# A conditioning matrix times two vectors, beside a two-block transformer on one core: 128x128 tiles with an fp32r split, or row chunks of 2048 columns in plain fp32

## What is computed

```python
silu_c = jax.nn.silu(c)                    # 1024 values
silu_cc = jax.nn.silu(c_ctx)               # 1024 values
for i in range(DEPTH):                     # 2
    mod_x = (silu_c @ w_mod[i] + b_mod[i])[:, None, :]     # w_mod[i] is 1024 x 3072
    mod_c = silu_cc @ w_mod[i] + b_mod[i]
    sh_x, sc_x, g_x = jnp.split(mod_x, 3, axis=-1)
    hx = rms_norm_2(x, norm_g[i]) * (1.0 + sc_x) + sh_x
    ...
    x = x + g_x * yx
```

## Time and profile before

| what | value |
|---|---|
| three runs | 1326.38, 1327.18, 1327.38 us; median 1327.18 us |
| profiled execution, first to last instruction | 1325.0 us (its own time outside the span is not listed; the median of the runs is 2.2 us above the span) |
| PE busy | 1271.4 us, 96% of the span |
| DVE, ACT, POOL busy | 945.7, 723.9, 391.0 us |
| chain that ended last | PE 78%, DVE 9%, ACT 7%, issue 3% |
| mean DMA rate | 145 GB/s |

### The profile page before, as it was taken

One profiled execution on the slowest core, in us unless ns is written; L12 is line 12 of the kernel. 1 busy time (PEld: TensorE's weight loads), 2 busy tenths in 40 slices (PEclk: granted clock), 3 DMA queues, 4 the chain that ended last, 5 costly groups with the idle time before them and its releaser, 6 DMA issues.

```text
span 1325.0 us, 24391 instructions
## 1 busy us (share of the span) xinstructions
PE 1271.4 (96%) x8908; PEld 1102.8 (83%) x8908; DVE 945.7 (71%) x1426; ACT 723.9 (55%) x1257; POOL 391.0 (30%) x377
## 2 busy tenths in 40 slices
PE   5999999999999999999999999999989999999996
PEld 4887899999999877898999998888855699987666
DVE  6878588888878985558988887853377548454674
ACT  5555455655567777545565657644366515413562
POOL 4942144545431140143445452011012320000022
PEclk9999999999999999999999999999999999999999
DMA  8565246666645542155576663322200274522100
GB/s 309 178 218 191 72 141 233 219 222 219 217 154 172 160 130 96 63 191 171 197 234 211 230 213 128 130 93 95 96 1 1 59 181 133 170 95 80 48 1 32
DMA packets 52665, 191.72 MB, mean 145 GB/s; under 512 B 6048, under 2 KB 6304, under 8 KB 52320
## 3 DMA queue, kind: packets, MB, share of 16 engines
q1 hardware_dynamic: 43488, 158.59, 36.2%
q0 software_dynamic: 8368, 31.33, 7.5%
q10 hardware_dynamic: 720, 0.57, 0.2%
HBM read 189.41 MB, written 1.05 MB: 144 GB/s over the span
## 4 chain that ended last, share of the span: by engine, by line
PE 78%; DVE 9%; ACT 7%; issue 3%; POOL 1%; DMA 1%; SPq 0%; DVEq 0%; ACTq 0%; POOLq 0%
PE G L417 13%; PE G L419 13%; PE G L418 13%; PE A L417 6%; PE A L419 6%; PE A L418 6%; DVE WL L1131 3%; PE R L651 3%; PE R L578 2%; PE R L558 2%; ACT WH L1848 2%; PE A L999 1%; PE R L417 1%; PE R L419 1%; PE R L418 1%
## 5 line engine op out<-in xcount | busy, mean ns | idle before, releaser
L1131 DVE TENSOR_TENSOR WL<-RAW,WH 128x1024 fp32r<-128x1024 f32 x295 | 390.4, 1330 | 245.3 <-ACT WH L1848 244.9
L1848 ACT ACTIVATE WH<-RAW 128x1024 fp32r<-128x1024 f32 x295 | 310.4, 1057 | 387.1 <-PE G L419 275.9
L417 PE MATMUL G<-XH,WH 128*128 128x256 f32 (+1 forms) x1336 | 398.7, 298 | 7.8 <-DVE WL L1131 4.6
L419 PE MATMUL G<-XH,WL 128*128 128x256 f32 (+1 forms) x1336 | 395.4, 296 | 0.0
L418 PE MATMUL G<-XL,WH 128*128 128x256 f32 (+1 forms) x1336 | 395.4, 296 | 0.0
L417 PEld LDWEIGHTS G<-XH,WH 128*128 128x128 f32 x1336 | 255.5, 191 | 21.6 <-issue 10.6
L418 PEld LDWEIGHTS G<-XL,WH 128*128 128x128 f32 x1336 | 255.6, 191 | 7.4
L419 PEld LDWEIGHTS G<-XH,WL 128*128 128x128 f32 x1336 | 255.7, 191 | 6.2
L417 PE MATMUL A<-HH,WH 128*128 128x256 f32 x352 | 99.9, 284 | 1.0 <-POOL HL L2477 1.0
L418 PE MATMUL A<-HL,WH 128*128 128x256 f32 x352 | 99.8, 283 | 0.0
L419 PE MATMUL A<-HH,WL 128*128 128x256 f32 x352 | 99.7, 283 | 0.0
(11 more groups left out here) (355 smaller groups left out, 2532.0 us busy)
## 6 DMA issues: line engine op xcount, KB each, us to landing
RAW<-in_wst SPq DMA_DIRECT2D x295, 512.0 KB, 4.1
M<-in_wmod POOLq DMA_DIRECT2D x48, 512.0 KB, 4.1
B<-in_rpb POOLq DMA_DIRECT2D x4, 1024.0 KB, 12.6
H<-in_x_t SPq DMA_DIRECT2D x2, 512.0 KB, 8.4
M<-in_x_tok SPq DMA_DIRECT2D x1, 1024.0 KB, 13.5
M<-in_ctx_t POOLq DMA_DIRECT2D x1, 1024.0 KB, 5.2
out_y<-M SPq DMA_DIRECT2D x2, 384.0 KB, 2.7
C<-in_cst SPq DMA_DIRECT2D x1, 737.0 KB, 15.1
```

Source lines behind the costliest of these rows:

```text
L417: mm(out, lh, rh, start=start, stop=False, skip_group_check=True)
L419: return mm(out, ll, rh, start=False, stop=stop, skip_group_check=True)
L1131: v.tensor_tensor(WL[:, slot, :], RAW[:, raw, :], WH[:, slot, :].bitcast(F32), ALU.subtract).then_inc(w_lo, 1)
L1848: act(WH[:, slot, :], RAW[:, raw, :], ACT.Copy).then_inc(w_hi, 1)
```

## The change

The matrix is cut in another way: 24 chunks of 128 rows by 2048 columns (1 MB each), eight to a third of the columns. A chunk is multiplied by four plain fp32 products of 512 columns, all with the same 128x32 vector, product g into the 32 array columns of group g (`modulate`). Eight chunks add up in `O` and give 2048 output columns.

- First attention: 8 chunks in place of 128 small products. Two stand ahead of the attention, one each in steps 2, 4, 6, 8, 10 and 12; none around the `heads_turn`. `RM` now has three slots of 1 MB.
- FFNs: 8 chunks each in place of 16 `refill`: one after tile 6, 8, 10, 12, 14, 16, 18 and 20. `SCR`, `RH`, `RL`, `YR`, and with them `high`, `row`, `rest`, are gone. Before each load POOL copies the chunk's vector (128x32) from `SC` to `SV`, so that PE can read it at a fixed address in its loop.
- After each FFN: one ACT copy of all of `O` and four transposes of 128 columns, instead of 16 small ones and a sum on DVE.

```diff
@@ program @@
-        SCR = sb("SCR", [P, KD, 32], F32R)
+        SV = sb("SV", [P, 2, 32])
-        RM = mv[:, 6144:12288].rearrange("p (s c) -> p s c", s=RMS)
+        RM = mv[:, 6144:12288].rearrange("p (s g c) -> p s g c", s=RMS, g=4)
@@ block.tensor @@
+            def modulate(vectors, buf, start, stop):
+                for g in range(4):
+                    m = mm(O[32 * g:32 * g + 32, :], vectors, RM[:, buf, g, :], start=start, stop=stop, skip_group_check=True)
+                m.then_inc(m_used, 1)
             def fill(n):
                 for _ in range(n):
-                    i, k = divmod(fills[0], KD)
+                    k = fills[0]
...
-                    g, q = i // 4, i % 4
-                    m = mm(out[32 * g:32 * g + 32, q * P:(q + 1) * P], SC[:, k, :], RM[:, i % RMS, k * P:(k + 1) * P],
-                           start=(k == 0), stop=(k == KD - 1), skip_group_check=True)
+                    pe.wait_ge(m_raw[k % RMS], 16 * (k // RMS + 1))
+                    modulate(SC[:, k, :], k % RMS, k == 0, k == CHUNKS - 1)
@@ attention @@
-                    if n < len(units) + 2:
-                        fill(filler)
+                    if n in filler:
+                        fill(1)
@@ around the first attention @@
-            fill(12)
+            fill(2)
             pe.wait_ge(bias_ok, 1)
-            attention("l0", scores_l0, value_l0, 5)
-            fill(14)
+            attention("l0", scores_l0, value_l0, range(2, 14, 2))
             heads_turn(0)
-            fill(6)
             heads_turn(1)
-            fill(6)
@@ ffn on PE @@
-                    if filled is not None:
-                        refill(layer, filled, i)
+                def modulated(buf, turn, start=False, stop=False):
+                    pe.wait_ge(r_vec[buf], turn + (v0 + 1))
+                    pe.wait_ge(r_raw[buf], turn * 16 + 16 * (v0 + 1))
+                    modulate(SV[:, buf, :], buf, start, stop)
                 for j in range(2, 7):
                     tile(j)
+                modulated(0, 0, start=True)
                 with pe.Fori(0, 3) as i:
-                    for d in range(4):
-                        tile(7 + d, i, d)
-                for d in range(3):
-                    tile(19 + d)
-                    refill(layer, d, 3)
+                    tile(7, i)
+                    tile(8, i)
+                    modulated(1, i)
+                    tile(9, i)
+                    tile(10, i)
+                    modulated(0, i + 1)
+                tile(19)
+                tile(20)
+                modulated(1, 3, stop=True)
+                tile(21)
                 down(0, p0 + 64, hb + FT - 1, p0 + 64, False, False)
-                refill(layer, 3, 3)
                 down(1, p0 + 65, hb + FT, p0 + 65, False, True)
@@ ffn on DVE and ACT @@
-                        rest(d, i)
...
-                        high(d, i)
@@ block.gpsimd @@
+                vectors = SC[:, k, :] if k < 2 else SC[:, bass.ds(i * 2 + k, 1), :].rearrange("p a c -> p (a c)")
+                g.tensor_copy(SV[:, k % 2, :], vectors).then_inc(r_vec[k % 2], 1)
...
+                gp.dma_start(RM[:, k % 2, :, :].rearrange("p g c -> p (g c)"), src).then_inc(r_raw[k % 2], 16)
...
             gp.wait_ge(t_mm, 1)
-            panels(0, 2)
+            chunks(0, 1)
             gp.wait_ge(t_mm, 2)
-            panels(2, 4)
+            chunks(1, 2)
             gp.wait_ge(bias_ok, 1)
+            chunks(2, 5)
...
             for h in range(8):
-                upto = min(PLAIN, 6 + (10 * h + 35) // 8)
-                panels(nextp, upto)
-                nextp = upto
+                if 1 <= h < 4:
+                    chunks(4 + h, 5 + h)
                 head_squares(h)
```

More of the change, by code:

```diff
@@ L330, in program @@
         sum_step = sem("sum_step")
-        r_raw = [sem(f"r_raw{i}") for i in range(4)]
-        r_hi, r_lo, r_y = sem("r_hi"), sem("r_lo"), sem("r_y")
+        r_raw = [sem(f"r_raw{i}") for i in range(2)]
+        r_vec = [sem(f"r_vec{i}") for i in range(2)]
         h_sq = sem("h_sq")
@@ L623, in advance, with attention @@
                     next(unit, None)
-            def attention(s, scores, value, filler=0, behind=None, meanwhile=(0, 0), first=0, last=None, ready=()):
+            def attention(s, scores, value, filler=(), behind=None, meanwhile=(0, 0), first=0, last=None, ready=()):
                 units = attn_units(s)
@@ L909, in _ @@
                                 + [(1, k) for k in range(8, 16)], T, lambda k: pe.wait_ge(at_g, AJ0["l1"] + k // 2 + 1))
-            attention("l1", scores_l1, value_l1, 0, first_o, (4, 3), first=2, ready=((1, TVALS),))
+            attention("l1", scores_l1, value_l1, (), first_o, (4, 3), first=2, ready=((1, TVALS),))
             advance(first_o, 32)
@@ L1025, in _ @@
             evacuated(pe, U0["a_z"] + 7)
-            attention("a", scores_a, value_a, 0, first_o, (2, 2), first=4)
+            attention("a", scores_a, value_a, (), first_o, (2, 2), first=4)
             advance(first_o, KD)
@@ L1099, in _ @@
             first_o = head_unit("b_o", [(c, k) for c in range(2) for k in range(7)] + [(0, 7), (1, 7)], T, lambda k: pe.wait_ge(at_o, AT_JOBS["a"] + k + 1))
[L1100 removed]
+            attention("b", scores_b, value_b, (), first_o, (6, 3), first=2, ready=((0, TVALS + 10), (1, TVALS + 12)))
             advance(first_o, 2 * KD)
@@ L2487, in ffn @@
                         hidden(d % 2, i * 4 + (hb + 6 + d), i * 12 + (p0 + 3 * d + 19))
-                        gathers(layer, 2 + d, i)
+                        if d % 2:
+                            gathers(layer, 2 + d // 2, i)
                 for j in range(18, FT):
                     hidden(j % 2, hb + j, p0 + 3 * j + 1)
-                    if j < 20:
-                        gathers(layer, j - 4, 0)
-            def panels(first, end):
-                for i in range(first, end):
-                    if i >= RMS:
-                        gp.wait_ge(m_used, i - RMS + 1)
-                    gp.dma_start(RM[:, i % RMS, :], wmod[i]).then_inc(m_raw[i % RMS], 16)
@@ L2501, in gathers, with chunks @@
-            def gathers(layer, n, i):
-                first = PLAIN * (layer + 1) + n
-                if n < 2:
-                    gp.wait_ge(m_used, PLAIN * (layer + 1))
-                else:
-                    gp.wait_ge(r_lo, i * 4 + (PLAIN * layer + n + 1))
-                src = wmod[bass.ds(i * 4 + first, 1)].rearrange("a p c -> p (a c)") if not isinstance(i, int) else wmod[first + 4 * i]
-                gp.dma_start(RR[:, n % 4, :], src).then_inc(r_raw[n % 4], 16)
+            def chunks(first, end):
+                for k in range(first, end):
+                    if k >= RMS:
+                        gp.wait_ge(m_used, k - RMS + 1)
+                    gp.dma_start(RM[:, k % RMS, :, :].rearrange("p g c -> p (g c)"), wmod[k]).then_inc(m_raw[k % RMS], 16)
```

111 lines of the change are left out of this document (31 added, 80 removed).

## The result

The changed kernel takes 1331.82 us (median of six runs, 1330.87 to 1334.18), the kernel before 1327.1 us (six runs, 1326.05 to 1328.14): a ratio of 1.0041, 95% interval 1.003 to 1.0052. It is slower by 4.7 us, 0.4%. The forecast was 1319.6 us, so the time lies inside the range of 1312 to 1336 but on the wrong side of no change, 12 us above the forecast. That it lies inside the range is luck: the upper end came from rival 3, a chunk of 2.0 us, and the chunk behaved as forecast.

What follows compares the result with a forecast made beforehand. PE, busy 96% of the span, was taken as the bound. FFNs -6.4, first attention +2.6, behind the attention -2.8, behind the FFNs -1.0: -7.6 us from 1325.0, so span 1317.4, median 1319.6 us, range 1312 to 1336.

Steps and rivals of the forecast that it cites:

- rival 3: Chunks: only two column groups run at a time, four rounds, 2.0 us a chunk, +8.7 us, 1336 us in all; chance 0.14.
- The chunk, four groups abreast: FFNs: a chunk's four products run side by side in two passes, 1.28 us a chunk, bounds 1.05 to 1.5.
- the sum for both FFNs: FFNs: 13.4 us a layer removed with the refills, 10.2 added by eight chunks; -3.2 a layer, -6.4 for both.
- so it is there at 105.3 or so: First attention: chunk 2, issued at 99.06, lands 6.4 us later, so DVE's unit 3 starts at 107.4 against 105.23, +2.2 us.
- 2.3 late, of which PE's new slack takes 1.1: First attention, step 8: chunk 5's load comes 2.3 us late, PE's slack absorbs 1.1, leaving +1.2; chunk 7 likewise +1.2.
- The DVE waits of -2.0: First attention after unit 3: DVE's 3.6 us of waits for PE, less some 1.5 at units 0 and 1, are saved.
- -2.8 behind the attention: After the first attention: without the fills the projection starts 2.8 us sooner, at 146.6 instead of 149.35; bounds -1.5 to -3.5.
- "Behind the FFNs" -1.0: After each FFN: four transposes cost 0.6 us where sixteen cost 1.1, -0.5 each, -1.0 for both.

Runs made afterwards that it cites:

- the first experiment: The changed kernel with the first attention's six chunks in steps 6, 8, ... 16 instead of 2, 4, ... 12: 1314.97 us, ratio 0.991 to the kernel before.

## Why the prediction was wrong

- **The chunk, four groups abreast: right.** It takes 1.19 us against 1.28, and the sum for both FFNs is -8.4 against -6.4. Of the 1.0 us more a layer, 8 x 0.09 = 0.7 come from the chunk and 0.2 from the end of the layer, where POOL's chain became 1.0 us shorter and not 0.8.
- **Chunk 2, "so it is there at 105.3 or so": mis-sized.** (99.06 + 6.4 is 105.5.) It landed 8.2 us after issue and not 6.4, where the 6.4 of the earlier trace rows was for two loads of half the size; even alone it takes 7.6, as the run with that load by itself shows. The chunk started at 107.09, +1.8. Then it ran at 1.2 GHz, and so did the scores behind it: from its start to DVE's unit 3 it took 110.63 - 107.09 = 3.5 us, not 1.28 + 0.25 + 0.6 = 2.1. Together +3.2 over the forecast: +5.4, not +2.2.
- **"2.3 late, of which PE's new slack takes 1.1": the step that failed worst.** The load was as fast as forecast (5.0 us from issue to landing, 5.2 taken). But its issue hangs on ACT's copy of head 0, and that copy keeps DVE's pace, as the chain above shows. PE came to step 8 at about 119.7, 2.7 us after that copy began (117.03), where before it had been 3.96. A PE that needs 1.2 us less for its own work arrives earlier at a load whose issue is no earlier, and waits longer: the saving had to be added to the 2.3, not taken from it, 3.5 in all; measured 3.37, and 3.87 at chunk 7. With the low clock behind the wait, which had no term either, the gap from unit 8 to 9 was 7.05 us (before 2.6) and from 12 to 13 7.49 (before 2.6): +4.4 and +4.9, where +1.2 each stood.
- **The DVE waits of -2.0** had the right sign and were too small: outside these two gaps the stage was 2.4 us shorter, and with all loads in time (the first experiment, and the one without loads) 3.1 and 4.0.
- **The clock had no term.** The page had a 9 in every slice of before, and the prediction took it as a state. It was the work of the fills, which filled every idle time of PE: with them back in the attention the mean clock is 0.997, without them it falls in the tail of every kernel run here, and in some at the attention's start. -2.8 behind the attention came as -2.3, but the first 27 products of the projection then ran at 0.21 us each and gave it all back, +2.6. No rival had this mechanism.
- **"Behind the FFNs" -1.0: a saving that is not on the chain that ends last.** The four transposes take 0.60 us against 1.18, but the next panel's `WL` was not ready sooner:

```profile
412.03 0.36 PE L411 MATMUL G<-XH,WH 128*128 128x256 f32 x1 [1.33 <-DVE WL L1113]
```

PE waited 0.41 us for the like product before. The 0.6 saved became a wait: DVE and ACT set this stage.

Of the 12.1 us between the forecast span (1317.4) and the measured one, the start takes 3.2, the stretch with chunks 5 and 7 takes 6.5 (6.9 - 0.4), the tail 0.5, the clock at the projection 2.6, the stages behind the FFNs 1.3, and the FFNs give back 2.0.

## What to carry to other kernels

When work is cut into larger pieces, ask of every load what its issue hangs on. If it hangs on another engine's pace, time saved on the engine that waits for the load lengthens the wait; what helped here was issuing earlier (11 us) or using later (four steps, 16 to 17 us). Filler work that hides in idle time also holds TensorE's clock up: before taking it away, look at what stands next on the chain that ends last, and leave a piece of it directly ahead of that.

## What the runs showed beyond that

- Four products of 512 columns in plain fp32, one per group of 32 columns, take 1.06 us together at 2.4 GHz, 1.94 at 1.2 GHz, and 3.62 at 2.4 GHz when they share one group.
- The clock also falls without a wait for any load: in the kernel without loads it was 1.00 up to 123 us and 0.50 from 131 to 139, where PE waited for DVE again and again and was busy 4.24 of 8 us.
- The same kernel, profiled twice, had the low clock in different stretches: the one of the first experiment lost 2.6 us against before at the start of the projection in one execution, and 1.9 there and 1.2 in FFN 0 in the other.
- A 1 MB load issued by POOL landed after 5.0 us with idle DMA engines and after 7.6 to 8.2 beside SP's panels.
